# mLSTM on one Trainium2 core: 28 of 64 sample state updates moved from the head loop into the second MLP

## The reference, cut to what matters

```
h     = (w_intra . v + w_inter * q @ C_old) / max(|den|, exp(-m))
C_new = decay * C_old + sum over 4 tokens of (k * w_state) v^T
n_new = decay * n_old + sum of k * w_state
```

```
x = x + rmsnorm(square(relu(rmsnorm(x) @ w_up)) @ w_down)
```

## Time and profile before

| what | value |
|---|---|
| median of 3 runs | 1106.06 us (1104.83 to 1107.03) |
| span of the profiled execution, first to last instruction | 1106.5 us |
| PE busy, PE weight loads busy | 1053.1 us (95%), 913.2 us (83%) |
| DVE, ACT, POOL busy | 653.9 us (59%), 530.0 us (48%), 184.5 us (17%) |
| moved by DMA | 261.23 MB, mean 236 GB/s |
| half-state loads, half-state stores | 64 and 64, 512 KB each |
| prompt-state stores, weight loads | 8 and 232, 512 KB each |

### The profile page before, as it was taken

How to read it: one execution, slowest core, us unless ns; L and a number is a source line. 1 busy time by engine, 2 the same in 40 slices (tenths; PEclk the granted TensorE clock), 3 DMA queues, 4 the chain that set the end, 5 groups by cost and what they waited for, 6 DMA issues and landing times.

```text
span 1106.5 us, 21578 instructions
## 1 busy us (share of the span) xinstructions
PE 1053.1 (95%) x8479; PEld 913.2 (83%) x8479; DVE 653.9 (59%) x960; ACT 530.0 (48%) x862; POOL 184.5 (17%) x250
## 2 busy tenths in 40 slices
PE   5999999899999999999899999899989999999995
PEld 5988778689999999998899945363529999999995
DVE  5567694643475543336996566767784485544333
ACT  5333654543566553435565344462624557553431
POOL 5134000000114220101400430412100104220100
PEclk9999999999999999999999999999989999999998
DMA  9799898999435445443743069999998435445431
GB/s 352 256 339 348 316 332 287 389 376 405 156 134 172 163 161 171 169 158 128 276 140 129 1 202 407 350 403 348 388 393 316 164 123 169 159 167 171 163 122 43
DMA packets 92762, 261.23 MB, mean 236 GB/s; under 512 B 8933, under 2 KB 10085, under 8 KB 92409
## 3 DMA queue, kind: packets, MB, share of 16 engines
q1 hardware_dynamic: 91818, 258.69, 65.0%
q0 software_dynamic: 432, 1.29, 0.4%
q10 hardware_dynamic: 432, 0.14, 0.1%
HBM read 218.36 MB, written 41.73 MB: 235 GB/s over the span
## 4 chain that ended last, share of the span: by engine, by line
PE 80%; DVE 10%; ACT 4%; issue 2%; POOL 2%; DMA 1%; SPq 1%; DVEq 0%; ACTq 0%
PE ps L2096 20%; PE ps L2097 20%; PE ps L2098 20%; PE ps L2208 2%; PE ps L2610 2%; PE ps L2571 2%; PE ps L2596 1%; PE ps L2289 1%; DVE cring L1787 1%; PE ps L2463 1%; DVE w_lo L1243 1%; PE ps L2190 1%; DMA w_raw<-in_weights 1%; DVE x L1328 1%; PE ps L2451 1%
## 5 line engine op out<-in xcount | busy, mean ns | idle before, releaser
L1243 DVE TENSOR_TENSOR w_lo<-w_raw,w_hi 128x1024 fp32r<-128x1024 f32 x232 | 286.5, 1241 | 209.8 <-ACT w_hi L718 209.1
L718 ACT ACTIVATE w_hi<-w_raw 128x1024 fp32r<-128x1024 f32 x232 | 242.4, 1054 | 209.9 <-PE ps L2098 173.2
L2096 PE MATMUL ps<-xin_hi,w_hi 128*128 128x288 f32 x1016 | 304.6, 300 | 14.8 <-DVE w_lo L1243 14.8
L2097 PE MATMUL ps<-xin_lo,w_hi 128*128 128x288 f32 x1016 | 301.5, 297 | 0.0
L2098 PE MATMUL ps<-xin_hi,w_lo 128*128 128x288 f32 x1016 | 301.2, 296 | 0.0
L2096 PEld LDWEIGHTS ps<-xin_hi,w_hi 128*128 128x128 f32 x1016 | 192.8, 190 | 26.6 <-DVE w_lo L1243 16.2
L2097 PEld LDWEIGHTS ps<-xin_lo,w_hi 128*128 128x128 f32 x1016 | 192.7, 190 | 0.7
L2098 PEld LDWEIGHTS ps<-xin_hi,w_lo 128*128 128x128 f32 x1016 | 192.6, 190 | 0.0
L2097 PE MATMUL ps<-hid_lo,w_hi 128*128 128x288 f32 x512 | 151.0, 295 | 0.0
L2098 PE MATMUL ps<-hid_hi,w_lo 128*128 128x288 f32 x512 | 150.9, 295 | 0.0
L2096 PE MATMUL ps<-hid_hi,w_hi 128*128 128x288 f32 x512 | 150.2, 293 | 0.0
(11 more groups left out here) (414 smaller groups left out, 1657.0 us busy)
## 6 DMA issues: line engine op xcount, KB each, us to landing
w_raw<-in_weights SPq DMA_DIRECT2D x232, 512.0 KB, 3.3
cring<-in_C SPq DMA_DIRECT2D x64, 512.0 KB, 6.4
out_Cs<-cring SPq DMA_DIRECT2D x64, 512.0 KB, 7.2
kv_a<-in_kv SPq DMA_DIRECT2D x56, 448.0 KB, 6.1
kv_b<-in_kv SPq DMA_DIRECT2D x52, 448.0 KB, 6.2
kv_w<-in_kv SPq DMA_DIRECT2D x20, 448.0 KB, 7.1
out_Cp<-cring SPq DMA_DIRECT2D x8, 512.0 KB, 7.0
out_v<-gaqkv SPq DMA_DIRECT2D x1, 1152.0 KB, 14.5
```

The lines of the kernel that those rows point to most:

```text
L718: act.activation(w_hi[:, l % UM], w_raw[:, l % W_SLOTS], ACT.Copy).then_inc(hi_ready, 1)
L1243: dve.tensor_tensor(w_lo[:, l % W_SLOTS], w_raw[:, l % W_SLOTS], w_hi[:, l % UM], ALU.subtract).then_inc(lo_ready, 1)
L2096: pe.matmul(out, w_hi[:, j, ws], hi, start=start and kk == 0, stop=False)
L2097: pe.matmul(out, w_hi[:, j, ws], lo, start=False, stop=False)
```

## The change

Seven pairs (head, p) are taken out of the head loop: p = 2, 3 of heads 1 and 2, and p = 1, 2, 3 of head 3. Each stands for two samples and two halves, so 28 of the 64 half states are formed later. In the head loop their old states are still loaded and multiplied with q, but `outers`, `new_state`, `own_values` and `c_store` are left out for them; their slot is free when PE has read it (`old_done`) instead of when a store has landed. Keys and values of heads 1 to 3 are written to a buffer in HBM (`keep`, six DMAs of 256 KB) and read back once (1.5 MB). Masks and decay columns are kept in SBUF (four small DVE copies). In UP1 and DOWN1, at 14 fixed steps (`LATE_AT`), PE runs four outer-product matmuls after the step, into banks 4 to 7; DVE forms one half state after each of the next two steps; SP loads the two old half states four steps ahead and stores the new ones three steps behind. ACT makes seven masked value copies. The loops of UP1 and DOWN1, and SP's from OUT_C on, are written out.

```diff
+LATER = {1: (2, 3), 2: (2, 3), 3: (1, 2, 3)}
+LATE_HEADS = sorted(LATER)
+LATE_VALUES = [(h, p) for h in LATE_HEADS for p in LATER[h]]
+LATE_PAIRS = [(h, p, half) for h, p in LATE_VALUES for half in range(2)]
+LATE_AT = [STEP0[UP1] + t for t in (7, 12, 17, 22, 27, 32, 36, 39, 42, 45, 48, 51, 54, 57)]
+LATE_SLOTS = [0, 1, 0, 1, 0, 1, 0, 2, 3, 1, 0, 2, 3, 1]
...
+        def slot_free(i):
+            j = i - C_SLOTS
+            if now(j):
+                return c_out[i % C_SLOTS], 16 * stores(i % C_SLOTS, i)
+            h, r = divmod(j, ITEMS)
+            b, half = ORDER[r]
+            return old_done, NB * h + ROUNDS.index((b % HALF_B, half)) + 1
...
                     if i >= C_SLOTS:
-                        sp.wait_ge(c_out[s], 16 * (i // C_SLOTS))
+                        sp.wait_ge(*slot_free(i))
...
             for i in range(NH * ITEMS):
                 if i == (NH - 1) * ITEMS:
                     sp.wait_ge(stage_full, use(NH - 2, "vs") + 1)
                     weights_back(0, 1)
-                if i == NH * ITEMS - 2:
-                    sp.wait_ge(hs_psum, NH)
-                    weights_back(2, 3)
-                if i == NH * ITEMS - 1:
-                    sp.wait_ge(c_mm, NH * ITEMS)
-                    weights_back(4, 5, 6)
-                c_store(i)
+                if i % ITEMS == 2 and i // ITEMS in LATER:
+                    keep_head(i // ITEMS)
+                if now(i):
+                    c_store(i)
                 if i + C_SLOTS - 2 < NH * ITEMS:
                     c_load(i + C_SLOTS - 2)
+            sp.wait_ge(old_done, NB * NH)
+            weights_back(2, 3)
+            sp.wait_ge(c_mm, outers_done(NH * ITEMS - 1))
+            sp.wait_ge(rows_kept, KEPT)
+            weights_back(4, 5, 6)
...
-            weight_rounds(STEP0[OUT_C] // W_SLOTS + 1, NSTEPS // W_SLOTS)
+            sp.wait_ge(y1s_full, 2)
+            sp.dma_start(kept.bitcast(F32), keep).then_inc(rows_kept, 16)
+            for t in range(STEP0[OUT_C], NSTEPS):
+                sp.wait_ge(step_done, t + 1)
+                if t + W_SLOTS < NSTEPS:
+                    weights(t + W_SLOTS, t % W_SLOTS)
+                if t + 4 in LATE_AT:
+                    late_loads(LATE_AT.index(t + 4))
+                if t - 3 in LATE_AT:
+                    late_stores(LATE_AT.index(t - 3))
...
+            def late_states(t):
+                for g in range(2):
+                    if t - g - 1 in LATE_AT:
+                        k = LATE_AT.index(t - g - 1)
+                        h, p, _ = LATE_PAIRS[k]
+                        s, nth = late_turn(k)
+                        dve.wait_ge(c_mm, NOW_ITEMS + k + 1)
+                        dve.wait_ge(*late_read(s, nth + 1))
+                        dve.scalar_tensor_tensor(late_ring[2 * s + g], late_ring[2 * s + g], late_decay[...],
+                                                 ps[:, 4 + 2 * g:6 + 2 * g, :], ALU.mult, ALU.add).then_inc(c_new, 1)
...
+            def late_outers(t):
+                if t not in LATE_AT:
+                    return
+                k = LATE_AT.index(t)
+                h, p, half = LATE_PAIRS[k]
+                if k == 0:
+                    pe.wait_ge(out_taken, OUT0[UP1] + OPEN)
+                    pe.wait_ge(std_ready, 7)
+                pe.wait_ge(vb_ready, NOW_VALUES + k // 2 + 1)
+                if k:
+                    pe.wait_ge(c_new, NOW_STATES + 2 * k)
+                for d in range(HD2):
+                    e = HD2 * half + d
+                    for g in range(2):
+                        own = slice(RG * g, RG * g + RG)
+                        last = pe.matmul(ps[:, 4 + 2 * g + d, :], kept[own, 2 * LATE_HEADS.index(h), P * e:P * e + P],
+                                         late_vb[own, (k // 2) % 2], start=True, stop=True)
+                last.then_inc(c_mm, 1)
...
                 p, half = ROUNDS[j]
+                if later(h, p):
+                    return
                 two = [item(h, p + HALF_B * g, half) for g in range(2)]
```

More of the change, by code:

```diff
@@ L314, in program @@
         hs, o = at("hs", o, NH, DH, parts=NS)
+        kept_at = o
         dups, o = at("dups", o, 2 * 2 * ET, 2 * NS)
@@ L560, in made @@
                 return p_new, 2 * h + half + 1
-            return c_new, 2 * NB * h + sum(1 for j in range(r + 1) if ORDER[j][0] < NB)
+            return c_new, sum(1 for j in range(i + 1) if now(j) and ORDER[j % ITEMS][0] < NB)
         def loads(i):
@@ L703, in _ @@
             for s in range(C_SLOTS):
-                sp.wait_ge(c_out[s], 16 * len(range(s, NH * ITEMS, C_SLOTS)))
+                sp.wait_ge(c_out[s], 16 * stores(s, NH * ITEMS))
+            for s in sorted(set(LATE_SLOTS)):
+                sp.wait_ge(*late_written(s, LATE_SLOTS.count(s)))
             sp.wait_ge(stored, 16 * 9)
@@ L732, in body @@
                         evac(it, l)
-                loop(act, UNITS[ph] // (2 * groups), body, peel_first=True, peel_last=True)
+                        if ph == DOWN1:
+                            late_values(base + 8 * groups * it + l)
+                n = UNITS[ph] // (2 * groups)
+                if ph == DOWN1:
+                    for it in range(n):
+                        body(it)
+                else:
+                    loop(act, n, body, peel_first=True, peel_last=True)
             def stat_squares(s, get, ready):
@@ L1218, in _ @@
                 for j, (p, half) in enumerate(ROUNDS):
-                    if half == 0 and p + 1 < HALF_B:
+                    if half == 0 and p + 1 < HALF_B and not later(h, p + 1):
                         own_values(h, p + 1)
@@ L1260, in body @@
                         evac(it, l)
-                loop(dve, UNITS[ph] // (2 * groups), body, peel_first=peel_first, peel_last=True)
+                        if ph in (UP1, DOWN1):
+                            late_states(base + 8 * groups * it + l)
+                n = UNITS[ph] // (2 * groups)
+                if ph in (UP1, DOWN1):
+                    for it in range(n):
+                        body(it)
+                else:
+                    loop(dve, n, body, peel_first=peel_first, peel_last=True)
             def scaled_out(ph, dst):
@@ L1910, in _ @@
                     for g in range(2):
-                        new_state(h, p + HALF_B * g, half)
+                        if not later(h, p):
+                            new_state(h, p + HALF_B * g, half)
                     chunk(h, j)
@@ L2669, in _ @@
                 for j in range(NB):
-                    last = old_state(h, j)
-                    if j == NB - 1:
-                        last.then_inc(hs_psum, 1)
+                    old_state(h, j)
                     if j == 2:
@@ L2686, in _ @@
             pe.wait_ge(y1s_ready, 1)
-            pe.wait_ge(*made(NH * ITEMS - 2))
+            pe.wait_ge(*made(max(i for i in range(NH * ITEMS) if now(i) and banks_of(i) == 0)))
             out_c(0)
```

125 lines of the change are left out of this document (107 added, 18 removed).

## The result

| kernel | median, us | runs | lowest to highest |
|---|---|---|---|
| before | 1106.06 | 5 | 1104.83 to 1107.03 |
| after | 1110.66 | 5 | 1109.18 to 1112.52 |

The ratio is 1.0042, with a 95% interval of 1.0030 to 1.0055. The change costs 4.6 us; I had forecast 1.9. That lies inside the range, 1103.3 to 1112. But by the bound that I had set, 0.2%, a difference of 0.42% is "slower", to which I had given 0.34, and not the "same" of the forecast, to which I had given 0.44.

A forecast was written before the change was run, and what follows sets the result against it. PE, busy 95% of the span, was taken as the bound. Gains of 3.3 + 2.1 + 4.5 = 9.9 us against 12.1 paid gave +2.1, taken over as +1.9 on 1106.06: 1107.9 us, range 1103.3 to 1112.

The forecast's parts named there:

- Head 1: Head loop: taking out its outer-product blocks in rounds 4 to 7 shortens this head by 3.3 us.
- head 2: Head loop: round 4 gives nothing because PE waits for `hs_diag`; rounds 5 to 7 give 2.1 us.
- Head 3 to OUT_C: End of the head loop: OUT_C starts at 823.9 instead of 830.83, the last load issued behind the prompt's second-half store.
- The clock at the tail: More PE idling makes 1.2 GHz certain in the tail; OUT_C's opening at half speed costs 2.4 us.
- rival 1: Tail: the clock holds or is back before OUT_C, so the change nets -1.5 us, 1104.5 us; chance 0.20.
- The blocks in the MLP: Second MLP: 14 outer-product blocks at 0.86 us each, entry and exit included, add 12.1 us to PE's path.
- rival 2: Second MLP: blocks do not overlap in pairs, 1.67 us each, net +13.4, 1119 us; chance 0.14 together with rival 4.
- rival 4: The change does not do what it says, for instance a late load holding DVE then PE; shares 0.14 with rival 2.
- At no cost: Second MLP: DVE updates, ACT's seven copies (at most 7 us), loads and stores are covered and add nothing.
- I take it over with +1.9: Whole kernel: the sum of +2.1 us on the 1106.5 span, carried to the 1106.06 median as +1.9, giving 1107.9.
- Signs: Expected: loop line x72, MLP line x56, no `w_lo` waits, MLP 12 us longer, OUT_C 12 earlier; under 9 or over 14 wrong.
- Rival 3: Head loop: the full DMA queue was the brake, earlier loads and stores give 5 us more, 1103 us; chance 0.08.

The follow-up runs named there:

- experiment 5: After, with the first value copy ahead of UP1's norm and only the last load ahead of the store of the prompt's second half; 1110.09 us, ratio 1.0021 to before.
- experiment 6: The kernel of experiment 5 plus unused matmuls where PE idled in head 2 and at the tail; 1105.90 us, ratio 0.9987 to before.
- experiment 9: Before, with the stores of the 28 half states cut to 8 of 128 partitions; 1107.07 us, ratio 0.9996 to before.
- experiment 10: After, with only eight half states of head 3 moved, first value copy ahead, loads in their old order, fillers at the tail; 1109.71 us, ratio 1.0023 to before.
- experiments 1: After, without the 56 outer-product matmuls in the second MLP and the waits for them; 1098.05 us, one run.
- 3: After, with ACT's first value copy moved ahead of UP1's norm; 1110.34 us, ratio 1.0037 to before.
- 2: After, with 8 of the 28 late loads and none of the late stores; 1114.70 us, one run.
- 4: After, with the load of item i + 8 issued ahead of the store of item i in the last head; 1114.56 us, ratio 1.0059 to before.

## Why the prediction came out as it did

- **Heads.** Head 1 was forecast at 3.3 and measured at 3.28; head 2 at 2.1 and 1.69, with the idle wait for `hs_diag` seen beforehand, but not that it is long enough for the clock to fall in part of the executions. Head 3 to OUT_C: 6.9 forecast, 6.43 measured, and by the mechanism named, the last load behind the store of the prompt's second half. It was issued at 809.84; the forecast's 813.8, shifted by what was measured ahead of head 3 (+0.92, -3.28, -1.69), is 809.75. The queue of the earlier trace rows was not as quiet as the prediction called it (DMA share 1.00 just before and 0.66 from 702 to 704), but the 4.8 us taken from it for that load came out at 5.1.
- **The clock at the tail.** Given back: 2.4 forecast, 1.47 measured. The low stretch was 6.8 us long and only its last 3.2 us lay in OUT_C. That more idling makes the low clock certain in the tail, as the prediction had it, is not borne out: experiment 5 idled for 2.06 us and more in its tail and kept 2.4 GHz, with OUT_C at 58.13 us. So rival 1's course happens by itself in some executions, and in experiment 6 it was had with fillers.
- **The blocks in the MLP.** 0.86 each: 12.1 forecast, 11.95 measured once the first wait is gone. The extra time around a block is there at the size of the earlier trace rows, and rival 2 (no overlap in pairs) did not happen. (Its price was a little high: two matmuls of the split block hold PE from 719.81 to 720.47, 0.66 us, not 0.73.)
- **The step that failed** is in "At no cost": "ACT: seven masked copies, ... at most 7 us on top of 99". The sum is right (0.71 us each) and says nothing of the first one, which stands behind ACT's work for the norm and UP1's first results and is due behind step 7. It cost 1.43 us. Priced by a mean over 204 us, the cover was there; at its own place it was not.
- **The transfer to the median.** "I take it over with +1.9" lowers the sum of +2.1 without a reason and set a span of 1106.5 beside a median of 1106.06. The run of after took 1.8 us more than its span, so that of before, by the same 1.8, would stand at 1108.3, above all five timed runs. Two scales were mixed.
- **Luck.** The spans differ by 4.17 us, 2.1 beyond the forecast sum. That small number is what is left of misses of both signs: 0.92 ahead of the heads, 1.43 for the first copy, 0.4 too much hoped for in head 2 and 0.5 in head 3, against 0.9 too much feared for the clock in OUT_C, 0.1 for the blocks and 0.25 at the end. The medians differ by 4.6; how that divides over executions in which the clock fell in head 2 and others was not measured for after itself.
- **Signs.** The loop has L2800 x72 and the MLP L2310 x56, PE never waits for `w_lo` in the MLP, which is 13.42 us longer (under the 14 that would have been wrong), and OUT_C begins 10.5 us earlier, where about 12 were forecast.
- **Rival 3**, the full queue as the brake, fell for heads 1 and 2 (experiment 9), as the argument from 0.3 us of waiting said. For head 3 it is half true: the queue is a limit there beside DVE (experiment 10).

Left open: what makes the clock fall in some executions and not in others; what the fillers would give the kernel before; and why the stretch ahead of the heads varies by 3.3 us over the profiled executions.

## What to carry to other kernels

Work moved out of a loop that is near several limits is worth what the loop loses at each place, not its own duration: here 28 half states cost 12 us where they went, and gave 5 in two heads and 6.4 in the last, where two limits had to fall together. Price a moved step's cover at the moment at which it is due; a mean over the stage hid a wait of 1.4 us. After removing work from PE, look for idle places that it leaves: filling them with unused matmuls lowered the median by 4.2 us, which neither order of the loads did. Fill them in the kernel before too, or the comparison gives the move what belongs to the fillers.

## What the hardware showed that was not expected

- The same idle time of 1.95 us in head 2 left the granted clock at 2.4 GHz in three profiled executions (after, experiments 1 and 3) and sent it to 1.2 GHz for 6.8 us in three others (2, 4 and 5), 2.9 us longer; ten runs of one kernel spread over 8.8 us with it and twelve over 2.5 us with fillers in it and in the tail.
- On the full queue of experiment 10 (402 GB/s) 512 KB land each 1.3 us, and a load takes 6.4 us in place of the 4.9 to 6.0 of the earlier trace rows; yet a head at a DMA share of 1.00 is as fast as one at 0.84 (48.81 and 48.80 us).
- In the MLP, neither more DMA traffic nor 28 updates of 1275 ns on DVE changed PE's pace by anything that can be measured: 217.69 us at a DMA share of 0.49 and 217.64 at 0.83, and without the blocks' matmuls, but with the updates and the DMAs, 204.19 us against the 204.22 of before.
